# Hybrid decoder trunk step: queries in residue, block and run order, K of the dense head group stored by blocks

## The chip, the cores and the metric

The kernel runs on the 8 NeuronCores of one Trainium2 chip. Every core works on two of the sixteen prompt sequences and on four of the thirty-two one-token samples, with no exchange between cores. The metric is the device time of the slowest core, in microseconds (us). A core has a matrix engine (TensorE: PE in the rows, PEld for its weight loads), VectorE (DVE), ScalarE (ACT), GpSimd (POOL) and SyncE (SP, which here only starts DMA transfers).

## The reference, cut to what matters

One layer: half a SwiGLU step, a mixing step, half a SwiGLU step, a final norm. The mixing step projects h = RMSNorm(x) once to a pooling input, to queries, keys and values of three head groups (four heads of 64 each) and to two gates.

```python
ATTN_GROUPS = ((128, 1), (512, 4), (2048, 16))  # (window, dilation)
q = apply_rope(qkv[:, :, g, 0], pos); k = apply_rope(qkv[:, :, g, 1], pos); v = qkv[:, :, g, 2]
o, lse = dilated_band_attention(q, k, v, window, dil)   # query t reads t - j*dil, j = 0..window//dil
wts = softmax(lses, axis=0); attn = einsum('gnlh,gnlhd->nlhd', wts, outs)
merged = sigmoid(gate_pool) * (pool @ w_pool_br) + sigmoid(gate_attn) * (attn @ w_attn_br)
x = x + merged @ w_o
```

The three groups of a head slot are merged by their softmax denominators. In the kernel the unnormalised products exp(score) times V of all three groups, and the sums of exp(score), are added up in one numerator and one denominator, and one division ends it.

## The kernel before, in words

**Tiles.** A sequence of 2048 tokens is four tiles of 512 tokens. Two tiles, A and B, make a pair, and the kernel runs four pairs one after the other: first feed-forward step for both, projections (`proj`), attention (`attn`), gates and `w_o`, second feed-forward step for both. Activations lie transposed: channels on the 128 partitions, the 512 tokens of the tile along the free dimension.

**Token order.** The 512 columns do not hold the tokens in their natural order. Column 32r + c holds a token of residue class r (of 16, modulo 16), and within a class the 32 tokens stand as c = 4 * c8 + u, where u (0 to 3) is the block of 128 tokens and c8 (0 to 7) the place of the token in that block's run. In the kernel's words this is the order "r c u". So the 128 tokens of block u stand at every fourth column: u, u+4, u+8, and so on.

**What each group reads.** Head group 0 (dilation 1, the dense group) needs blocks of 128 neighbouring tokens, group 1 (dilation 4) needs 128 columns of one class modulo 4, which stand side by side, group 2 (dilation 16) needs 32 columns of one class modulo 16, also side by side. `col` in `attn` (line 755) says so: a slice with step 4 for group 0, a contiguous slice of 128 for group 1. Group 2 slices in `unit2` by itself.

**Attention.** `unit01` handles two heads of one group against the current or the previous block of keys. It issues 16 score matmuls (4 blocks, 2 halves of the head, 2 heads; K is the stationary operand, Q the moving one, 32 partitions each), ScalarE takes exp of the two banks into `pbuf`, VectorE multiplies by a mask (line 765), then come 8 matmuls with V that add into the numerator bank, and 2 matmuls with ones that add into the denominator bank. `unit2` does the same for group 2. The units of a tile are a generator, and `merge` interleaves them by a table of costs with other matmul work: the attention of tile A with the projection of tile B, the attention of tile B with the gates and `w_o` of tile A. Each engine works through its own queue in program order.

**Rotary step.** `rope_pair` (lines 576 to 585) turns two PSUM banks into two rotated halves on VectorE: four products into `rtmp`, then two sums into `qT`, into `kT0`/`kT1`, or into the float32 buffer `kf` where K is also an output of the kernel (group 2 always, groups 0 and 1 in the last tile of a sequence). From `kf` ScalarE copies into the K buffer (lines 682 and 685) and a DMA stores it. All matmuls are recorded at line 198, whoever issues them, so rows are told apart by tile names: scores read `sb_qT` and `sb_kT`, numerator matmuls `sb_pbuf` and `sb_V`, denominator matmuls `sb_pbuf` and `sb_ones`.

**End of a head pair.** ScalarE takes Ln and Exp of the denominators (lines 857 and 859), VectorE multiplies numerator, 0.5 and reciprocal into `attnT` (line 861). GpSimd computes the pooling branch meanwhile.

Of the kernel before, what the change touches and what calls it, by code (L numbers as in the profile page):

```python
# [215 lines left out]
def build(cfg=CFG):  # L216
# [30 lines left out]
    with K.es:  # L247
# [328 lines left out]
        def rope_pair(bA, bB, seg, outA, outB, t, resA, resB):  # L576
# [64 lines left out]
        def proj(seg, s, t, i, mx, S=None):  # L641
# [25 lines left out]
            def qk(g, isk):  # L667
# [4 lines left out]
                if not isk:  # L672
                    rope_pair(bA, bB, seg, qT[:, 2 * g, :], qT[:, 2 * g + 1, :], rtmp, [qT.r[2 * g]], [qT.r[2 * g + 1]])
                else:
                    kout = (g == 2) or last
                    kres = [kTg[g].r[t if g == 2 else t % 3]]
                    if not kout:
                        rope_pair(bA, bB, seg, kTg[g][:, t % 3, 0, :], kTg[g][:, t % 3, 1, :], rtmp, kres, kres)
                    else:
                        rope_pair(bA, bB, seg, kf[:, 0, :], kf[:, 1, :], rtmp, [kf.r[0]], [kf.r[1]])  # L680
                        if g == 2:
                            act.op(lambda: nc.scalar.copy(out=kT2[:, :, :].rearrange("p a (r t c) -> p a r t c", r=NR, t=NTILE)[:, :, :, t, :],
                                                          in_=kf[:, :, :].rearrange("p a (r c) -> p a r c", c=NI)), reads=kf.r, writes=kres)
                        else:
# [64 lines left out]
        def attn(t, i):  # L749
# [5 lines left out]
            def col(g, u, tt=None):  # L755
                return slice(u, T, 4) if g == 0 else slice(u * 128, (u + 1) * 128)
# [27 lines left out]
            def unit01(g, c, which):  # L784
# [8 lines left out]
                if not units:  # L793
# [6 lines left out]
                scores(bk, [lambda i, b, u=u, tt=tt, ku=ku, ab=ab: (ps[b][:, u * 128:(u + 1) * 128], kb[hr(i), tt % 3, ab, col(g, ku)],  # L800
                                                                   qT[hr(i), 2 * g + ab, col(g, u)], ab == 0, ab == 1)
# [27 lines left out]
            def unit2(c):  # L829
# [15 lines left out]
                for part in range(2):  # L845
# [10 lines left out]
                    if part == 1:  # L856
                        act.op(lambda: nc.scalar.activation(out=rden[c][:, :], in_=ps[denb[c]][:, :], func=AF.Ln), reads=[psr[denb[c]]],
# [404 lines left out]
def _consts():  # L1262
# [4 lines left out]
    for g, o in enumerate(order):  # L1267
        mask01[:, g, 0] = o[:, None] >= o[None, :]
        mask01[:, g, 1] = o[:, None] <= o[None, :]
    mask2 = (_run(np.arange(128) % 32)[:, None] <= _run(np.arange(32))[None, :]).astype(np.float32)  # L1270
# [110 lines left out]
```

How the kernel before makes its waits and increments, by code:

```python
    def wait_tok(self, tok):  # L66
        sem, val = tok
        if sem is self.sem:
            if self.is_pe:
                return
            assert val <= self.cnt, (self.name, val, self.cnt)
        if self.known.get(id(sem), 0) >= val:
            return
        self.eng.wait_ge(sem, val)
        self.known[id(sem)] = val
# [21 lines left out]
    def op(self, fn, reads=(), writes=(), inc=True):  # L97
        self.nops = getattr(self, "nops", 0) + 1
        self.wait_deps(reads, writes)
        ins = fn()
        if inc:
            ins.then_inc(self.sem, 1)
            self.cnt += 1
            tok = (self.sem, self.cnt)
        else:
            tok = (self.sem, self.cnt + 1)
        self.commit(tok, reads, writes)
        return tok
# [1 line left out]
    def dma(self, out, in_, dsem, reads=(), writes=(), **kw):  # L110
        self.wait_deps(reads, writes)
        self.eng.dma_start(out=out, in_=in_, **kw).then_inc(dsem.sem, 16)
        dsem.total += 16
        tok = (dsem.sem, dsem.total)
        self.commit(tok, reads, writes)
        return tok
```

## Time and profile before

| what | us |
|---|---|
| median of 3 runs | 2925.41 (2922.5 to 3424.03) |
| profiled execution, whole | 2923.13 |
| profiled execution, span of the slowest core (core 4) | 2921.9 |
| spans of the eight cores | 2911.1 to 2921.9 |
| TensorE busy on that core | 2815.1 (96%) |
| VectorE busy | 1038.7 (36%) |
| ScalarE busy | 755.7 (26%) |
| GpSimd busy | 331.0 (11%) |

The span is the time from a core's first to its last instruction in one profiled execution, and the whole of that execution is 1.2 us longer. Busy time is summed over a core's instructions. The mean granted TensorE clock of core 4 is 0.987 of full speed. An engine that is busy for a third of the span can still be the one that is waited for in a certain stretch.

### The profile page before, as it was taken

What the parts mean: (1) busy time and instruction counts of PE and PEld (TensorE: products, weight loads), DVE (VectorE), ACT (ScalarE), POOL (GpSimd) and SP (SyncE); (2) the same over time, 40 slices, a digit from 0 to 9 for tenths busy, and PEclk for the clock granted to TensorE, in tenths of its full rate; (3) what the DMA queues carried; (4) which work ended last, traced back from release to release, by engine and by line L of the source; (5) the groups of instructions that cost most, each with busy time, mean ns of one, the idle gap of its engine ahead of it and who ended that gap; (6) DMA issues with size and microseconds to landing.
All of it is one profiled execution on the core that took longest, in us unless ns stands there. A gap on an engine that the chain in (4) does not pass through costs nothing.

```text
span 2921.9 us, 47174 instructions; the slowest of 8 cores (2911.1 to 2921.9 us)
## 1 busy us (share of the span) xinstructions
PE 2815.1 (96%) x16993; PEld 1350.6 (46%) x17306; DVE 1038.7 (36%) x1704; ACT 755.7 (26%) x1340; POOL 331.0 (11%) x448
## 2 busy tenths in 40 slices
PE   7999988999999999999999999999999999999997
PEld 2444544444444455444444445444444445544443
DVE  3212753421241166442142128542124216644112
ACT  2111233312121124421122113432112112442111
POOL 1000620000000044000000007000000004400000
PEclk8999998999999999999999999999999999999999
DMA  9666765765353334343343424344224223433221
GB/s 212 146 150 134 192 150 139 182 171 139 107 173 107 110 125 153 109 146 127 103 152 110 138 80 149 125 131 148 83 75 165 71 89 119 144 118 114 73 75 70
DMA packets 97089, 372.58 MB, mean 128 GB/s; under 512 B 12472, under 2 KB 14168, under 8 KB 93660
## 3 DMA queue, kind: packets, MB, share of 16 engines
q1 hardware_dynamic: 75760, 270.81, 27.7%
q0 software_dynamic: 17648, 86.94, 13.9%
q10 hardware_dynamic: 3456, 11.80, 1.0%
q8 instruction: 145, 2.38, 0.3%
q14 instruction: 80, 0.66, 0.1%
HBM read 342.66 MB, written 99.03 MB: 151 GB/s over the span
## 4 chain that ended last, share of the span: by engine, by line
PE 89%; DVE 4%; issue 3%; DMA 2%; ACT 1%; ACTq 0%; SPq 0%; DVEq 0%; POOL 0%; POOLq 0%
PE ps L198 89%; DMA sb_xT<-x 1%; DVE sb_hT L507 1%; DMA sb_uexs<-spoolT 1%; DVE sb_ystg L507 1%; DMA kp<-sb_kf 1%; DVE sb_rtmp L579 1%; DVE sb_pbuf L765 0%; DVE sb_V L214 0%; DVE sb_kf L579 0%; DVE sb_kf L917 0%; ACT sb_pbuf L761 0%; ACT sb_V L213 0%; DMA sb_kT<-kcs 0%; DVE sb_mergedT L919 0%
## 5 line engine op out<-in xcount | busy, mean ns | idle before, releaser
L198 PE MATMUL ps<-sb_hT,sb_w 128*128 128x512 bf16 x7461 | 1685.2, 381 | 31.6 <-issue 6.3
L198 PEld LDWEIGHTS ps<-sb_hT,sb_w 128*128 128x128 bf16 x7680 | 740.6, 98 | 920.2 <-issue 61.0
L525 ACT ACTIVATE sb_stmp<-ps 128x512 f32<-128x512 f32 x352 | 209.8, 597 | 920.5 <-PE ps L198 871.2
L198 PE MATMUL ps<-sb_actTB,sb_w 128*128 128x512 bf16 x1371 | 316.6, 379 | 1.8
L198 PE MATMUL ps<-sb_actTA,sb_w 128*128 128x512 bf16 x1382 | 316.2, 379 | 1.8 <-DVE sb_actTs L526 0.2
L468 ACT ACTIVATE sb_sq<-sb_xT 128x512 bf16<-128x512 f32 x224 | 139.4, 630 | 666.7 <-DVE sb_xT L570 467.3
L526 DVE TENSOR_TENSOR sb_actTB<-sb_stmp,ps 128x512 bf16<-128x512 f32 x176 | 120.9, 687 | 485.8 <-PE ps L198 472.3
L526 DVE TENSOR_TENSOR sb_actTA<-sb_stmp,ps 128x512 bf16<-128x512 f32 x176 | 119.9, 686 | 421.1 <-PE ps L198 417.1
L570 DVE SCALAR_TENSOR_TENSOR sb_xT<-ps,sb_xT 128x512 f32<-128x512 f32 x128 | 87.8, 690 | 434.3 <-PE ps L198 421.2
L198 PEld LDWEIGHTS ps<-sb_actTA,sb_w 128*128 128x128 bf16 x1408 | 136.9, 98 | 163.7 <-issue 0.2
L198 PEld LDWEIGHTS ps<-sb_actTB,sb_w 128*128 128x128 bf16 x1408 | 136.7, 98 | 163.7
L507 DVE SCALAR_TENSOR_TENSOR sb_hT<-sb_xT,sb_gains,sb_rstd 128x512 bf16<-128x512 f32 x192 | 140.3, 798 | 82.1 <-ACT sb_rstd L499 58.3
L579 DVE TENSOR_TENSOR sb_rtmp<-ps,sb_rope 128x512 f32<-128x512 f32 x192 | 119.6, 678 | 17.6 <-PE ps L198 17.3
L917 DVE SCALAR_TENSOR_TENSOR sb_kf<-sb_kf,ps 128x512 f32<-128x512 f32 x128 | 82.5, 683 | 112.5 <-PE ps L198 104.3
L198 PE MATMUL ps<-sb_mergedT,sb_w 128*128 128x512 bf16 x495 | 118.1, 379 | 4.1 <-issue 1.6
L765 DVE TENSOR_TENSOR sb_pbuf<-sb_pbuf,sb_mask 128x512 bf16<-128x512 bf16 (+2 forms) x152 | 79.3, 538 | 116.1 <-ACT sb_pbuf L761 113.3
L112 POOL DMA_DIRECT2D sb_w<-wch x95 | 50.7, 537 | 577.5 <-PE ps L198 553.1
L112 POOL DMA_DIRECT2D kvs<-c x40 | 19.6, 490 | 828.5 <-PE ps L198 801.9
L198 PE MATMUL ps<-sb_sq,sb_meanm 128*128 128x512 bf16 x252 | 88.6, 385 | 15.9 <-ACT sb_sq L468 10.9
L761 ACT ACTIVATE sb_pbuf<-ps 128x512 bf16<-128x512 f32 (+4 forms) x152 | 81.7, 594 | 57.6 <-PE ps L198 52.6
L198 PE MATMUL ps<-sb_w,sb_hT 128*128 128x256 bf16 x768 | 92.8, 278 | 0.7 <-DVE sb_rtmp L579 0.7
L198 PEld LDWEIGHTS ps<-sb_w,sb_hT 128*128 128x128 bf16 x768 | 77.4, 105 | 14.6 <-issue 4.8
(134 smaller groups left out, 1528.5 us busy)
## 6 DMA issues: line engine op xcount, KB each, us to landing
sb_w<-wscr SPq DMA_DIRECT2D x341, 512.0 KB, 4.0
sb_w<-wch POOLq DMA_DIRECT2D x83, 512.0 KB, 8.3
wscr<-sb_w SPq DMA_DIRECT2D x83, 512.0 KB, 4.5
sb_w<-wscr SPq DMA_DIRECT2D x52, 384.0 KB, 3.5
kvs<-c POOLq DMA_DIRECT2D x32, 511.8 KB, 5.0
y<-sb_ystg POOLq DMA_DIRECT2D x7, 2048.0 KB, 12.1
sb_xT<-x SPq DMA_DIRECT2D x8, 1024.0 KB, 11.9
sb_xT<-x SPq DMA_DIRECT2D x4, 2048.0 KB, 10.8
```

Source lines behind the costliest of these rows:

```text
L112: self.eng.dma_start(out=out, in_=in_, **kw).then_inc(dsem.sem, 16)
L198: self.pe.op(lambda: self.nc.tensor.matmul(out, lhsT, rhs, start=start, stop=stop, **kw), reads=reads, writes=writes, inc=inc)
L468: act.op(lambda: nc.scalar.activation(out=sq[:, 0:n], in_=seg.xT[:, c, 0:n], func=AF.Square), reads=[seg.xT.r[c]], writes=sq.r)
L507: dve.op(lambda c=c: nc.vector.scalar_tensor_tensor(out=dst[:, c, 0:n], in0=seg.xT[:, c, 0:n], scalar=gains[:, gi, c:c + 1], in1=seg.rstd[ ...
L525: act.op(lambda: nc.scalar.activation(out=st[:, 0:n], in_=ps[bg][:, 0:n], func=AF.Silu), reads=[psr[bg]], writes=st.r)
L526: dve.op(lambda: nc.vector.tensor_tensor(out=seg.actT[:, j, 0:n], in0=st[:, 0:n], in1=ps[bu][:, 0:n], op=ALU.mult), reads=st.r + [psr[bu]] ...
L570: dve.op(lambda: nc.vector.scalar_tensor_tensor(out=seg.xT[:, m, 0:n], in0=ps[b][:, 0:n], scalar=0.5, in1=seg.xT[:, m, 0:n], op0=ALU.mult, ...
L579: tt = lambda o, a, b, op, rd, wr: dve.op(lambda: nc.vector.tensor_tensor(out=o, in0=a, in1=b, op=op), reads=rd, writes=wr)
L761: act.op(lambda: nc.scalar.activation(out=pb[0:rows, c0:c1], in_=ps[b][0:rows, c0:c1], func=AF.Exp, scale=0.125), reads=[psr[b]], writes=pb.r)
L765: dve.op(lambda: nc.vector.tensor_tensor(out=pv, in0=pv, in1=mask.unsqueeze(1).broadcast_to(list(pv.shape)), op=ALU.mult), reads=pb.r + mr ...
L917: dve.op(lambda: nc.vector.scalar_tensor_tensor(out=gt[:, k, 0:n], in0=gt[:, k, 0:n], scalar=1.0, in1=ps[bk][:, 0:n], op0=ALU.add, op1=ALU ...
```

## The change

The queries of all three groups are written in the order "r u c" (class, block, place in the run) instead of "r c u". K of group 0 is written in the order "u r c", so each block of 128 tokens is contiguous; K of groups 1 and 2 stay as they were. The numerator and denominator banks therefore have their columns in the order "r u c". The last VectorE operation of a head pair writes `attnT` back in the order "r c u", so that everything behind attention is as before. The factor 0.5 moves into the Ln (scale 2.0). The masks of group 1 and 2 are renumbered on the query side. The number of instructions changes only where K of group 0 goes through `kf` (the last tile of each sequence): one ScalarE copy of 1024 columns becomes two of 512.

```diff
+        nat = lambda ap: ap.rearrange("p (r c u) -> p r c u", c=8, u=4)
+        def rope_pair(bA, bB, seg, outA, outB, t, resA, resB, order=None):
...
+            pi = nat if order else (lambda ap: ap)
+            po = (lambda ap: ap.rearrange("p (%s) -> p r c u" % order, c=8, u=4)) if order else pi
...
-            tt(outA, t[:, 0, 0:n], t[:, 1, 0:n], ALU.subtract, [t.r[0], t.r[1]], resA)
-            tt(outB, t[:, 2, 0:n], t[:, 3, 0:n], ALU.add, [t.r[2], t.r[3]], resB)
+            tt(po(outA), pi(t[:, 0, 0:n]), pi(t[:, 1, 0:n]), ALU.subtract, [t.r[0], t.r[1]], resA)
+            tt(po(outB), pi(t[:, 2, 0:n]), pi(t[:, 3, 0:n]), ALU.add, [t.r[2], t.r[3]], resB)
...
-                    rope_pair(..., qT[:, 2 * g, :], qT[:, 2 * g + 1, :], rtmp, ...)
+                    rope_pair(..., qT[:, 2 * g, :], qT[:, 2 * g + 1, :], rtmp, ..., "r u c")
...
-                        rope_pair(..., kTg[g][:, t % 3, 0, :], kTg[g][:, t % 3, 1, :], rtmp, kres, kres)
+                        rope_pair(..., kTg[g][:, t % 3, 0, :], kTg[g][:, t % 3, 1, :], rtmp, kres, kres, "u r c" if g == 0 else None)
...
+                        elif g == 0:
+                            for ab in range(2):
+                                act.op(lambda: nc.scalar.copy(out=kT0[:, t % 3, ab, :].rearrange("p (u r c) -> p r c u", c=8, u=4), in_=nat(kf[:, ab, :])), ...)
...
-            def col(g, u, tt=None):
-                return slice(u, T, 4) if g == 0 else slice(u * 128, (u + 1) * 128)
+            def col(ap, g, u):
+                return ap.rearrange("p (r u c) -> p u r c" if g == 0 else "p (u r c) -> p u r c", u=4, c=8)[:, u]
...
-                        K.mm(ps[numb[c]][64 * i:64 * i + 64, col(g, u)], vs[k][0][:, h * 64:(h + 1) * 64], pbs[i][:, u * 128:(u + 1) * 128],
+                        K.mm(col(ps[numb[c]][64 * i:64 * i + 64, :], g, u), vs[k][0][:, h * 64:(h + 1) * 64], col(pbs[i][:, :], 1, u),
...
-                    den = den.rearrange("p (i u) -> p u i" if g == 0 else "p (u i) -> p u i", u=4)[:, u0:u1, :]
+                    den = den.rearrange("p (r u c) -> p u r c" if g == 0 else "p (u r c) -> p u r c", u=4, c=8)[:, u0:u1]
...
-                        dve.op(lambda: nc.vector.scalar_tensor_tensor(out=attnT[:, c, :], in0=ps[numb[c]][:, :], scalar=0.5, in1=rden[c][:, :], ...
+                        dve.op(lambda: nc.vector.tensor_tensor(out=attnT[:, c, :].rearrange("p (r c u) -> p r u c", c=8, u=4),
+                                                               in0=tok(ps[numb[c]][:, :]), in1=tok(rden[c][:, :]), op=ALU.mult),
```

In bytes along a partition: the moving Q of a group 0 score was read at a step of 8 bytes, and is now read in runs of 8 columns (16 bytes) every 64 bytes; the stationary K was loaded at a step of 8 bytes, and is now contiguous; the numerator and denominator of group 0 were written in PSUM at a step of 16 bytes (one float32 each), and are now written in runs of 8 float32 (32 bytes) every 128 bytes. On VectorE, consecutive bf16 elements of a query sum now go 16 bytes apart (they were 2 bytes apart), those of a group 0 K sum 256 bytes apart, and those of `attnT` 8 bytes apart.

No instruction changes its place; what changes is the form in which operands are walked. VectorE, the rotary step of tile A of the first pair, in which q0, k0 (`sb_kT_22`), q1, k1 and so on follow each other:

```order
-L579 TENSOR_TENSOR sb_rtmp<-ps,sb_rope 128x512 x4
-L579 TENSOR_TENSOR sb_qT_94<-sb_rtmp 128x512 x2
-L579 TENSOR_TENSOR sb_kT_22<-sb_rtmp 128x512 x2
-L579 TENSOR_TENSOR sb_kT_23<-sb_rtmp 128x512 x2
+L584 TENSOR_TENSOR sb_rtmp<-ps,sb_rope 128x512 x4
+L584 TENSOR_TENSOR sb_qT_94<-sb_rtmp 128x16x8x4 x2
+L584 TENSOR_TENSOR sb_kT_22<-sb_rtmp 128x128x4 x2
+L584 TENSOR_TENSOR sb_kT_23<-sb_rtmp 128x512 x2
```

The two sums of each query, and those of K of group 0, are now walked in rows of 4 elements; the products and K of group 1 are as before. TensorE, the numerator and denominator matmuls of one group 0 unit of the same tile:

```order
-L198 MATMUL ps<-sb_pbuf_97,sb_V_25 64x128
-L198 MATMUL ps<-sb_pbuf_98,sb_V_25 64x128
-L198 MATMUL ps<-sb_pbuf_97,sb_ones 64x4x128
+L198 MATMUL ps<-sb_pbuf_97,sb_V_25 64x16x8
+L198 MATMUL ps<-sb_pbuf_98,sb_V_25 64x16x8
+L198 MATMUL ps<-sb_pbuf_97,sb_ones 64x4x16x8
```

Their outputs go in 16 runs of 8 columns for each block. Matmuls of groups 1 and 2 keep their forms.

## Rows read from the trace of the kernel before

**Rows 1.** The page: span, TensorE's busy time, shares of the chain that ended last.
```profile
span 2921.9 us, 47174 instructions; the slowest of 8 cores (2911.1 to 2921.9 us)
PE 2815.1 (96%) x16993; PEld 1350.6 (46%) x17306; DVE 1038.7 (36%) x1704; ACT 755.7 (26%) x1340; POOL 331.0 (11%) x448
PE 89%; DVE 4%; issue 3%; DMA 2%; ACT 1%; ACTq 0%; SPq 0%; DVEq 0%; POOL 0%; POOLq 0%
```
**Rows 2.** TensorE's timeline: start, us, count; group 0 scores, then group 1 scores.
```profile
1118.18 1.10 PE L198 MATMUL ps<-sb_qT,sb_kT 32*128 32x128 bf16 x16
...
1164.19 0.62 PE L198 MATMUL ps<-sb_qT,sb_kT 32*128 32x128 bf16 x16
```
**Rows 3.** TensorE's timeline: numerator and denominator of group 0, then of group 1.
```profile
1160.07 0.63 PE L198 MATMUL ps<-sb_pbuf,sb_V 128*64 128x128 bf16 x8
1160.49 0.64 PE L198 MATMUL ps<-sb_pbuf,sb_ones 128*64 128x512 bf16 x2
1161.06 1.90 PE L198 MATMUL ps<-sb_hT,sb_w 128*128 128x512 bf16 x8
...
1173.07 0.41 PE L198 MATMUL ps<-sb_pbuf,sb_V 128*64 128x128 bf16 x8
1173.32 0.38 PE L198 MATMUL ps<-sb_pbuf,sb_ones 128*64 128x512 bf16 x2
1173.64 1.90 PE L198 MATMUL ps<-sb_hT,sb_w 128*128 128x512 bf16 x8
```
**Rows 4.** VectorE's groups by form, whole span: count, busy us, mean ns.
```profile
L919 DVE TENSOR_TENSOR sb_mergedT<-sb_kf 128x512 bf16<-128x512 f32 x64 | 44.3, 692 | 8.1 <-DVE sb_kf L917 3.2
L579 DVE TENSOR_TENSOR sb_qT<-sb_rtmp 128x512 bf16<-128x512 f32 x48 | 43.3, 941 | 0.0
L579 DVE TENSOR_TENSOR sb_kT<-sb_rtmp 128x512 bf16<-128x512 f32 x24 | 32.9, 1372 | 1.2
L579 DVE TENSOR_TENSOR sb_kf<-sb_rtmp 128x512 f32<-128x512 f32 x24 | 16.0, 706 | 0.0
L526 DVE TENSOR_TENSOR sb_actTs<-sb_stmps,ps 128x4 bf16<-128x4 f32 x44 | 6.8, 155 | 4.1 <-ACT sb_stmps L525 4.0
```
**Rows 5.** The query sums alone: duration ns min/median/max.
```profile
L579 DVE TENSOR_TENSOR sb_qT<-sb_rtmp x48: 670/708/1797, 301.4 to 2535.6; 128x512 bf16<-128x512 f32 x48
```
**Rows 6.** VectorE's timeline, projection of tile A, second pair; brackets: idle before, releaser.
```profile
1065.05 2.47 DVE L579 TENSOR_TENSOR sb_rtmp<-ps,sb_rope 128x512 f32<-128x512 f32 x4
1067.44 1.41 DVE L579 TENSOR_TENSOR sb_qT<-sb_rtmp 128x512 bf16<-128x512 f32 x2
...
1080.72 3.16 DVE L579 TENSOR_TENSOR sb_kT<-sb_rtmp 128x512 bf16<-128x512 f32 x2
...
1093.72 1.28 DVE L579 TENSOR_TENSOR sb_kf<-sb_rtmp 128x512 f32<-128x512 f32 x2
1097.33 0.92 DVE L765 TENSOR_TENSOR sb_pbuf<-sb_pbuf,sb_mask 128x512 bf16<-128x512 bf16 x2 [2.32 <-ACT sb_pbuf L761]
```
**Rows 7.** GpSimd's timeline beside it.
```profile
1080.81 6.17 POOL L615 TENSOR_TENSOR sb_wtmp<-sb_wtmp 128x896 f32<-128x896 f32 x3
```
**Rows 8.** ScalarE's timeline behind it.
```profile
1095.09 1.05 ACT L682 CAST sb_kT<-sb_kf 128x1024 bf16<-128x1024 f32 x1 [6.82 <-DVE sb_kf L579]
1096.62 1.10 ACT L761 ACTIVATE sb_pbuf<-ps 128x512 bf16<-128x512 f32 x2
```
**Rows 9.** TensorE's timeline behind it: two group 0 scores, then the numerator.
```profile
1091.10 1.10 PE L198 MATMUL ps<-sb_qT,sb_kT 32*128 32x128 bf16 x16
1093.97 1.11 PE L198 MATMUL ps<-sb_qT,sb_kT 32*128 32x128 bf16 x16
1098.49 0.63 PE L198 MATMUL ps<-sb_pbuf,sb_V 128*64 128x128 bf16 x8 [1.58 <-DVE sb_pbuf L765]
```
**Rows 10.** Waits of TensorE for masks: us in total, times, longest us.
```profile
PE ps L198 <- DVE sb_pbuf L765: 18.6, 8, 8.2
```
**Rows 11.** VectorE and TensorE in the projection of tile B: mask, then its numerator.
```profile
1131.40 1.22 DVE L765 TENSOR_TENSOR sb_pbuf<-sb_pbuf,sb_mask 128x512 bf16<-128x512 bf16 x2
...
1134.11 0.63 PE L198 MATMUL ps<-sb_pbuf,sb_V 128*64 128x128 bf16 x8
```

More of the change, by code:

```diff
@@ L672, in qk @@
                 if not isk:
[L673 removed]
+                    rope_pair(bA, bB, seg, qT[:, 2 * g, :], qT[:, 2 * g + 1, :], rtmp, [qT.r[2 * g]], [qT.r[2 * g + 1]], "r u c")
                 else:
@@ L677, in qk @@
                     if not kout:
-                        rope_pair(bA, bB, seg, kTg[g][:, t % 3, 0, :], kTg[g][:, t % 3, 1, :], rtmp, kres, kres)
+                        rope_pair(bA, bB, seg, kTg[g][:, t % 3, 0, :], kTg[g][:, t % 3, 1, :], rtmp, kres, kres, "u r c" if g == 0 else None)
                     else:
@@ L683, in qk @@
                                                           in_=kf[:, :, :].rearrange("p a (r c) -> p a r c", c=NI)), reads=kf.r, writes=kres)
+                        elif g == 0:
+                            for ab in range(2):
+                                act.op(lambda: nc.scalar.copy(out=kT0[:, t % 3, ab, :].rearrange("p (u r c) -> p r c u", c=8, u=4), in_=nat(kf[:, ab, :])),
+                                       reads=kf.r, writes=kres)
                         else:
@@ L799, in unit01 @@
                 cc[0] = c
-                scores(bk, [lambda i, b, u=u, tt=tt, ku=ku, ab=ab: (ps[b][:, u * 128:(u + 1) * 128], kb[hr(i), tt % 3, ab, col(g, ku)],
-                                                                   qT[hr(i), 2 * g + ab, col(g, u)], ab == 0, ab == 1)
+                scores(bk, [lambda i, b, u=u, tt=tt, ku=ku, ab=ab: (col(ps[b][:, :], 1, u), kb[hr(i), tt % 3, ab, ku * 128:(ku + 1) * 128],
+                                                                   col(qT[hr(i), 2 * g + ab, :], g, u), ab == 0, ab == 1)
                             for (u, tt, ku) in units for ab in range(2)], kres + qT.r[2 * g:2 * g + 2])
@@ L856, in unit2 @@
                     if part == 1:
-                        act.op(lambda: nc.scalar.activation(out=rden[c][:, :], in_=ps[denb[c]][:, :], func=AF.Ln), reads=[psr[denb[c]]],
+                        act.op(lambda: nc.scalar.activation(out=rden[c][:, :], in_=ps[denb[c]][:, :], func=AF.Ln, scale=2.0), reads=[psr[denb[c]]],
                                writes=rden[c].r)
@@ L860, in unit2 @@
                                writes=rden[c].r)
-                        dve.op(lambda: nc.vector.scalar_tensor_tensor(out=attnT[:, c, :], in0=ps[numb[c]][:, :], scalar=0.5, in1=rden[c][:, :],
-                                                                      op0=ALU.mult, op1=ALU.mult), reads=[psr[numb[c]], ] + rden[c].r,
-                               writes=[attnT.r[c]])
+                        tok = lambda ap: ap.rearrange("p (r u c) -> p r u c", c=8, u=4)
+                        dve.op(lambda: nc.vector.tensor_tensor(out=attnT[:, c, :].rearrange("p (r c u) -> p r u c", c=8, u=4),
+                                                               in0=tok(ps[numb[c]][:, :]), in1=tok(rden[c][:, :]), op=ALU.mult),
+                               reads=[psr[numb[c]]] + rden[c].r, writes=[attnT.r[c]])
                         K.give(denb[c])
@@ L1266, in _consts @@
     mask01 = np.zeros((128, 2, 2, 128), np.float32)
[L1267 to L1270, printed above, removed]
+    qorder = (order[0], 4 * (pos % 32) + pos // 32)
+    for g, (o, q) in enumerate(zip(order, qorder)):
+        mask01[:, g, 0] = o[:, None] >= q[None, :]
+        mask01[:, g, 1] = o[:, None] <= q[None, :]
+    mask2 = (_run(np.arange(128) % 32)[:, None] <= np.arange(32)[None, :]).astype(np.float32)
     half = 32
```

3 lines of the change are left out of this document (1 added, 2 removed).

## The prediction

> **What bounds the kernel now.** I read the page first. TensorE is busy for 2815.1 of 2921.9 us, and the chain that ended last runs through it for 89% [rows 1]. So time on TensorE counts one for one nearly everywhere, and time on another engine counts only where TensorE is seen to wait for it. Next I read TensorE's timeline in the attention stretches, because the change touches only attention. Two units that do the same arithmetic on the same shapes have different lengths there. Sixteen score matmuls of the dense group take 1.10 us, sixteen of group 1 take 0.62 [rows 2]. Eight numerator and two denominator matmuls take 0.99 us of the engine in the dense group (1160.07 to 1161.06) and 0.57 in group 1 (1173.07 to 1173.64) [rows 3]. The only difference between the two is how operands and outputs are walked. Last I read who keeps TensorE waiting. Masks do so 8 times, for 18.6 us [rows 10], and I followed one of these back through ScalarE to VectorE [rows 6, 8, 9], since VectorE is where the change adds work.
>
> **TensorE's part.** A full dense unit can save 1.10 - 0.62 = 0.48 us in its scores [rows 2] and 0.99 - 0.57 = 0.42 us in numerator and denominator [rows 3], together 0.90. There are 8 tiles, 2 head pairs and 2 kinds of unit (current and previous block), so 32 units. In the first tile of each of the two sequences the previous block is missing for one of four blocks: 4 units are three quarters long. That makes 28 x 0.90 + 4 x 0.75 x 0.90 = 27.9 us at full recovery. Whether recovery is full the trace does not show, since no row has runs of 8. The lower bound is nothing: runs with gaps could be as slow as single columns with gaps. The upper bound is group 1's price, as the arithmetic is the same and group 1's operands have no gaps. I take the upper bound. K is now exactly as contiguous as in group 1, a run of 8 touches no more memory words than the same 8 columns without gaps do, if words are 16 bytes of Q or 32 bytes of PSUM wide or less, and the matmuls before touched several times as many. The skill speaks partly against it: the Trainium skill, Advanced Engine Details and Errata, section Memory Cachelines, says that any PSUM pattern that is not contiguous slows matmuls much, and a line later that pairs of neighbours are enough. The first of these sentences would leave the 0.42 in place, which is a rival below.
>
> **What of it is not seen in the end.** In each pair two dense score units stand right before the place where TensorE waits for a mask that is late for another reason [rows 9]. Being through 2 x 0.48 = 0.96 us sooner there only lengthens the wait of 1.58. This pattern occurs four times, once a pair, and the longest mask wait, 8.2 us in the first pair [rows 10], also stands behind two dense score units. Five times 0.96 is 4.8 us. What remains is 27.9 - 4.8 = 23.1 us.
>
> **VectorE's part.** The 48 query sums and 12 of the sums into K (group 0, the six tiles that are not last) are written with gaps, and 16 attnT products. In length they stay 512 elements. What a write with gaps costs on VectorE no row shows. A contiguous sum of two float32 operands into bf16 takes 692 to 708 ns [rows 4, 5]; the same with four columns takes 155, so the 512 elements account for about 540. The lower bound of the added cost is 0 (the engine handles one element at a time in float32, whatever the addresses; the same sum with a float32 output, twice the bytes, takes 706, so written bytes are not its limit) [rows 4]. The upper bound by the longest such row is 1797 ns [rows 5], or 1.09 us more. That one waited for something, so I keep it as an end only. I take 0, because the price of these sums has so far followed the element count alone.
>
> Why this matters although VectorE is busy for 36% only: in the projection of tile A it works without a gap from the first product at 1065.05 to the end of the kf sum at 1095.00, 40 instructions; its first idle time is in front of the mask at 1097.33 [rows 6]. Behind the kf sum wait ScalarE's copy of K (6.82 us idle before it) and, in ScalarE's queue behind that copy, the exps of the two dense units [rows 8], behind them the masks, and behind these TensorE [rows 9]. So there every ns added to VectorE reaches TensorE. Eight permuted sums stand in that stretch (six of queries, two of K of group 0), in each of four pairs: 32 sums. In the other stretches there is cover: in the projection of tile B a mask is ready at 1132.62 and used at 1134.11 [rows 11], 1.49 us later, and two sums more expensive by up to 0.7 us each stay within it. In the gates there are no such sums. If the cover of 1.49 were gone, each us would count there too, in 6 to 8 sums a pair.
>
> **The rest.** attnT: same count, contiguous reads, one instruction per head pair, 8 bytes step; the scalar 0.5 moves into an activation that is there anyway: 0. Two ScalarE copies of 512 instead of one of 1024, twice in the kernel: one fixed cost each, below 0.2 us, in a queue that idles. Masks and DMAs are the same in number and size. SP's and POOL's queues are passed by nothing. A slower VectorE sum holds up GpSimd and the reverse: the K sums into bf16 average 1372 ns against 692, and the one at 1080.72 (3.16 us for two) ran beside GpSimd's additions [rows 4, 6, 7]. That is there before, and it only grows if the sums do.
>
> **Sum.** 2923.1 (the profiled execution) - 23.1 = 2900.0. The median of the runs is 2.3 us above that execution, so the forecast for the median is **2902 us**.
>
> **The rivals.**
> *Half rate on VectorE.* Writes of single bf16 elements 16 bytes apart run at half rate: 0.54 us more each. For it: TensorE shows in the same memory that gaps nearly double a pass (1.10 against 0.62). Against it: TensorE handles a column in far less time than VectorE an element, so memory may keep up with VectorE. In the 32 sums without cover that is 32 x 0.54 = 17.3 us, so 2902 + 17 = 2919. The Trainium skill, Advanced Engine Details and Errata, section Memory Cachelines, speaks for this: it wants two hits in every 16 byte line of SBUF, and a query sum now has one. No run here shows it yet. By the same sentence Q read at 8 bytes had its two hits and should have been fast; the dense scores cost 1.10, so either K's load was slow or the rule is too kind.
> *Runs in PSUM stay slow.* Only the scores recover: 30 or so units x 0.48 = 14.9, less 4.8: 10.1 us, so 2915; if the scores stay slow as well, 2925.
> *Slower than before.* VectorE becomes the bound of the tile A projection: each sum takes two more passes of 0.54, so 1.08 more. The 32 sums cost 34.6 us; in tile B's projection 2.16 per query exceeds the cover of 1.49 by 0.67, some 12 times, 8 us; the sum is 2902 + 43 = 2945. The point from which this side decides is 23.1 / 32 = 0.72 us more per sum. For it: the stretch has no slack at all, and longer sums also hold up GpSimd. Against it: nothing in the trace is three times as slow for its addresses alone.
>
> **Chances and range.** Forecast (VectorE within 0.15 us of its old price, full recovery) 46%, 2897 to 2907. Half rate 28%, 2914 to 2924. Runs in PSUM stay slow, wholly or in part, 14%, 2909 to 2925. Slower than before 10%. Something else 2%. A range of 2896 to 2926 leaves out the slower case and a little at both ends. The lower end is full recovery with a little less lost in waits. A measurement of this kernel can tell about 2% (58 us) from no change. The whole dense excess is 27.9 us, so faster by over 2% needs something not seen here: 1%. Slower by over 2% needs more than 2.5 us per uncovered sum: 2%. Within 2%: 97%.
>
> **What would show it.** In the trace of the changed kernel, dense scores should take 0.62 for sixteen, and numerator plus denominator 0.57; 0.99 there means runs in PSUM stay slow. The query sums should have a median near 708 ns and the tile A projection of the second pair should reach its kf sum 30 us after the first product; near 1250 ns, and 34 us, it is the half rate. The mask wait behind it should be about 2.5 us instead of 1.58 if VectorE is unchanged. I am wrong if query sums exceed 1.4 us, or if TensorE's waits for masks grow beyond some 45 us in all.

## The result: 2.7% slower, and the profile after

The changed kernel takes 1.0268 times as long as before (95% interval 1.0245 to 1.0292): about 3002 us against a median of 2924.7, so some 78 us more where I forecast 23 less. Two of its four executions (3240.9 and 3419.0 us) had one die at a clock of 0.82 to 0.89, which happens to the kernel before too (3424.0); the ratio leaves such executions out.

The page of the changed kernel, to be held against [rows 1]:
```profile
span 3001.5 us, 47178 instructions; the slowest of 8 cores (2993.2 to 3001.5 us)
PE 2815.0 (94%) x16993; PEld 1343.8 (45%) x17306; DVE 1146.2 (38%) x1704; ACT 761.0 (25%) x1342; POOL 380.7 (13%) x448
PE 84%; DVE 7%; issue 5%; ACT 2%; DMA 2%; SPq 0%; DVEq 0%; ACTq 0%; POOL 0%; POOLq 0%
```
TensorE is as busy as before (2815.0 against 2815.1), so all of the 79.6 us show as idle time of TensorE: 106.8 before (2921.9 - 2815.1), 186.5 now. (Why its busy time did not fall is a question of its own, answered below.) VectorE is busy for 107.5 us more.

Did TensorE's walks get faster? Its timeline in two stretches at full clock: sixteen scores of group 0, then numerator and denominator of group 0 and the projection behind them, to be held against the group 0 rows of [rows 2, 3]:
```profile
1145.64 0.62 PE L198 MATMUL ps<-sb_qT,sb_kT 32*128 32x128 bf16 x16
...
1170.81 0.41 PE L198 MATMUL ps<-sb_pbuf,sb_V 128*64 128x128 bf16 x8
1171.06 0.38 PE L198 MATMUL ps<-sb_pbuf,sb_ones 128*64 128x512 bf16 x2
1171.38 1.90 PE L198 MATMUL ps<-sb_hT,sb_w 128*128 128x512 bf16 x8
```
Yes, as forecast: scores 0.62 for 1.10, numerator and denominator 0.57 (1170.81 to 1171.38) for 0.99. By form the three groups fell from 52.7, 32.1 and 31.3 us to 41.5, 26.2 and 24.7: 23.7 us in all.

VectorE, grouped by form, and the query sums alone (ns min/median/max), against [rows 4, 5]:
```profile
L584 DVE TENSOR_TENSOR sb_qT<-sb_rtmp 128x512 bf16<-128x512 f32 x48 | 124.0, 2776 | 0.0
L584 DVE TENSOR_TENSOR sb_kT<-sb_rtmp 128x512 bf16<-128x512 f32 x24 | 53.8, 2242 | 1.2
L872 DVE TENSOR_TENSOR sb_attnT<-ps,sb_rden 128x512 bf16<-128x512 f32 x16 | 21.2, 1326 | 30.8 <-ACT sb_rden L869 30.7
```
```profile
L584 DVE TENSOR_TENSOR sb_qT<-sb_rtmp x48: 2387/2627/4072, 302.0 to 2618.9; 128x512 bf16<-128x512 f32 x48
```
The shortest query sum takes 2387 ns, above every one of before (670 to 1797). These three groups carry 80.7 + 20.9 + 10.2 us more (attnT, the last VectorE operation of a head pair, was 11.0 us, 689 ns each).

Who keeps TensorE waiting (us in total, times, longest), against [rows 10]:
```profile
PE ps L198 <- DVE sb_rtmp L584: 50.9, 17, 9.1
PE ps L198 <- DVE sb_pbuf L775: 23.0, 9, 9.0
PE ps L198 <- DVE sb_attnT L872: 14.9, 10, 4.3
...
PE ps L198 <- ACT sb_pbuf L771: 7.8, 3, 3.9
PE ps L198 <- ACT sb_kf L913: 7.1, 5, 4.4
```
In the kernel before these were 3.6, 18.6, none, 0.2 and 5.0, so they grew by 47.3, 4.4, 14.9, 7.6 and 2.1: 76.3 of the 79.7 us by which TensorE's idle time grew. The first is not the wait that I had followed. sb_rtmp is the output of the rope products, and they are what reads the projection out of its PSUM bank. Behind a long sum the products come late, the banks stay taken, and TensorE has nowhere to write.

The same place as in [rows 6, 9], the tile A projection of the second pair. VectorE:
```profile
1078.80 2.47 DVE L584 TENSOR_TENSOR sb_rtmp<-ps,sb_rope 128x512 f32<-128x512 f32 x4
1081.20 4.76 DVE L584 TENSOR_TENSOR sb_qT<-sb_rtmp 128x512 bf16<-128x512 f32 x2
...
1088.17 5.93 DVE L584 TENSOR_TENSOR sb_kT<-sb_rtmp 128x512 bf16<-128x512 f32 x2
...
1103.24 4.49 DVE L584 TENSOR_TENSOR sb_kT<-sb_rtmp 128x512 bf16<-128x512 f32 x2
1107.66 2.47 DVE L584 TENSOR_TENSOR sb_rtmp<-ps,sb_rope 128x512 f32<-128x512 f32 x4
...
1119.85 1.28 DVE L584 TENSOR_TENSOR sb_kf<-sb_rtmp 128x512 f32<-128x512 f32 x2
```
TensorE beside it:
```profile
1110.27 1.01 PE L198 MATMUL ps<-sb_qT,sb_kT 32*128 32x128 bf16 x15 [4.72 <-DVE sb_rtmp L584]
1111.21 3.59 PE L198 MATMUL ps<-sb_hT,sb_w 128*128 128x512 bf16 x8
1114.74 1.03 PE L198 MATMUL ps<-sb_qT,sb_kT 32*128 32x128 bf16 x16
1120.46 3.19 PE L198 MATMUL ps<-sb_hT,sb_w 128*128 128x512 bf16 x7 [4.69 <-DVE sb_rtmp L584]
1124.63 0.64 PE L198 MATMUL ps<-sb_pbuf,sb_V 128*64 128x128 bf16 x8 [0.97 <-DVE sb_pbuf L775]
```
From the first product to the end of the kf sum VectorE needs 42.3 us without a gap, 30.0 before: 12.4 more. From each start to the next, 11.3 of them stand in the eight permuted sums, and 1.3 in the two sums of K of group 1, whose form did not change (4.49 at 1103.24, 3.16 before [rows 6]). GpSimd, which works beside them, is busy for 380.7 us in the whole kernel instead of 331.0: that longer sums would hold GpSimd up as well was in the prediction. TensorE stops twice, until a product frees a bank (the first time at 1107.66 + 2.47 = 1110.13, and it goes on at 1110.27). The mask at the end, which I had expected to carry the cost, is waited for by 0.97 us only: the time has been lost ahead of it. The second effect stands between the stops: eight 512-column matmuls take 3.59 us, where eight of the same shape take 1.90 in [rows 3]. The windows of that stretch (us, PE, PEld, DVE, ACT, POOL busy, TensorE clock, DMA share, GB/s) show why, first two of after, then one of before around the same place (it begins further ahead of the first product):
```profile
1076.00:1126.00 50.00, 39.16 (x235) 21.83 (x237) 46.70 (x46) 10.66 (x20) 34.83 (x29) 0.86 0.38 126
1110.27:1114.74 4.47, 4.47 (x24) 1.78 (x25) 4.47 (x2) 0.00 (x0) 0.84 (x1) 0.50 0.00 0
```
```profile
1057.00:1100.00 43.00, 41.05 (x262) 24.13 (x266) 39.69 (x52) 11.58 (x22) 32.12 (x34) 1.00 0.49 164
```
After the 4.72 us stop the granted clock is 0.50, the lower of the two levels (1.2 GHz). Behind the stop of 1.58 us in the kernel before [rows 9] it stayed at 1.00. Over the whole kernel the mean clock of a core was 0.987 at least, and is now 0.975 at most. So 22.0 of the 23.7 us that TensorE saved were spent again as slower matmuls (the hT,w group 1685.2 → 1702.6 us, w,hT 92.8 → 97.4), which is why its busy time did not move.

### The profile page after: what moved, and what is told of

The parts are those of the page before. It is cut to its first block, busy times and chain, and to the rows that moved or that the text cites. A ratio compares the mean times of both kernels' runs of the same rounds, so it can differ in the third digit from the quotient of the medians.

```text
span 3001.5 us, 47178 instructions; the slowest of 8 cores (2993.2 to 3001.5 us)
## 1 busy us (share of the span) xinstructions
PE 2815.0 (94%) x16993; PEld 1343.8 (45%) x17306; DVE 1146.2 (38%) x1704; ACT 761.0 (25%) x1342; POOL 380.7 (13%) x448
## 4 chain that ended last, share of the span: by engine, by line
PE 84%; DVE 7%; issue 5%; ACT 2%; DMA 2%; SPq 0%; DVEq 0%; ACTq 0%; POOL 0%; POOLq 0%
PE ps L198 84%; DVE sb_rtmp L584 1%; DVE sb_hT L507 1%; DVE sb_qT L584 1%; DVE sb_pbuf L775 1%; DMA sb_uexs<-spoolT 1%; DVE sb_ystg L507 1%; DVE sb_kT L584 1%; DMA kp<-sb_kf 0%; DMA sb_xT<-x 0%; DVE sb_V L214 0%; DVE sb_attnT L872 0%; ACT sb_pbuf L771 0%; DVE sb_kf L928 0%; DVE sb_kf L584 0%
## 5 line engine op out<-in xcount | busy, mean ns | idle before, releaser
L198 PE MATMUL ps<-sb_hT,sb_w 128*128 128x512 bf16 x7461 | 1702.6, 384 | 52.4 <-DVE sb_rtmp L584 19.5
L584 DVE TENSOR_TENSOR sb_qT<-sb_rtmp 128x512 bf16<-128x512 f32 x48 | 124.0, 2776 | 0.0
L198 PE MATMUL ps<-sb_qT,sb_kT 32*128 32x128 bf16 (+4 forms) x1968 | 62.9, 202 | 41.9 <-DVE sb_rtmp L584 25.0
L198 PE MATMUL ps<-sb_w,sb_hT 128*128 128x256 bf16 x768 | 97.4, 286 | 2.5 <-DVE sb_rtmp L584 2.5
```

The costliest lines, as they stand in the source:

```text
L198: self.pe.op(lambda: self.nc.tensor.matmul(out, lhsT, rhs, start=start, stop=stop, **kw), reads=reads, writes=writes, inc=inc)
```

## The experiments

My theory after the result: a bf16 write on VectorE whose neighbours in time lie 16 bytes apart costs 1.7 us more per 512 elements, and the sums alone make the loss. Rivals: the many short rows of the access pattern cost it (each row now has 4 elements); or something else in the change (K's copies, attnT, the new matmul walks) does.

**e1_forms: each form by itself.** The kernel before, with 17 forms in a row behind its end, four times:
```diff
+        for _ in range(4):
+            dve.op(... tensor_tensor(out=oo, in0=tA_, in1=tB_, op=ALU.add))                  # contiguous
+            dve.op(... out=P(oo, "c r u", "r c u"), in0=P(tA_, "r c u", "r c u"), ...)       # rows of 4, neighbours
+            dve.op(... out=P(oo, "r u c", "r c u"), in0=P(tA_, "r c u", "r c u"), ...)       # rows of 4, 16-byte step
+            ...
```


> The kernel before, with a list of VectorE and ScalarE instructions of 512 elements in different walks put behind its end, four times over, when no other engine works (its total time is not of interest; what it adds after the end belongs to no output). Two theories of why a query sum went from 0.70 to 2.4 us at least. Step theory: a bf16 element that is written alone, 16 bytes or more from the last, costs some 3.4 ns more; the length of a row does not matter. Then rows of 64 elements with a 16 byte step take 2.4 us as well, rows of 128 with an 8 byte step about 1.3, and rows of 4 whose elements are neighbours stay at 0.69. Row theory: every innermost row costs some 13 ns to set up, whatever its steps. Then rows of 4 neighbours take 2.4 us, rows of 8 neighbours 1.5, and long rows with any step stay at 0.69. Permuted reads with contiguous writes: the step theory leaves open what reads cost, the row theory says 1.5 us in rows of 8.


Measured (ns min/median/max; in order: contiguous; rows of 4 neighbours; the query form; 8-byte step; 4-byte step; inputs read at a 16-byte step; float32 written at a 32-byte step):
```profile
L1247 DVE TENSOR_TENSOR sb_kT<-sb_rtmp x4: 693/694/694, 2913.0 to 2986.2; 128x512 bf16<-128x512 f32 x4
L1248 DVE TENSOR_TENSOR sb_kT<-sb_rtmp x4: 692/692/693, 2913.8 to 2987.0; 128x512 bf16<-128x512 f32 x4
L1250 DVE TENSOR_TENSOR sb_kT<-sb_rtmp x4: 2385/2385/2387, 2915.3 to 2988.6; 128x512 bf16<-128x512 f32 x4
L1252 DVE TENSOR_TENSOR sb_kT<-sb_rtmp x4: 1296/1296/1300, 2920.4 to 2993.6; 128x512 bf16<-128x512 f32 x4
L1253 DVE TENSOR_TENSOR sb_kT<-sb_rtmp x4: 727/727/729, 2921.8 to 2995.0; 128x512 bf16<-128x512 f32 x4
L1255 DVE TENSOR_TENSOR sb_kT<-sb_rtmp x4: 1062/1062/1062, 2925.1 to 2998.3; 128x512 bf16<-128x512 f32 x4
L1258 DVE TENSOR_TENSOR sb_kf<-sb_rtmp x4: 1065/1065/1067, 2928.8 to 3002.0; 128x512 f32<-128x512 f32 x4
```
Short rows cost nothing (692), so that rival is dead. The 16-byte step costs 1.69 us, as the step theory had it, and a larger step no more: two further forms, rows of 64 at 16 bytes and rows of 4 at 256 bytes, took 2.42 and 2.43. It is the same on ScalarE (16-byte step, then contiguous):
```profile
L1261 ACT CAST sb_kT<-sb_rtmp x4: 2416/2416/2416, 2931.6 to 3004.8; 128x512 bf16<-128x512 f32 x4
L1262 ACT CAST sb_kT<-sb_rtmp x4: 617/617/617, 2934.1 to 3007.3; 128x512 bf16<-128x512 f32 x4
```

**e2_plain_writes and e3_only_query_writes: the two halves of the change.** e2 keeps every new matmul walk and writes contiguously (K's copy and attnT too); e3 is the kernel before, with the new rope writes only.
```diff
 # e2, against the changed kernel
-            pi = nat if order else (lambda ap: ap)
-            po = (lambda ap: ap.rearrange("p (%s) -> p r c u" % order, c=8, u=4)) if order else pi
+            pi = lambda ap: ap
+            po = pi
 # e3, against the kernel before
-            tt(outA, t[:, 0, 0:n], t[:, 1, 0:n], ALU.subtract, ...)
+            tt(po(outA), pi(t[:, 0, 0:n]), pi(t[:, 1, 0:n]), ALU.subtract, ...)
```


> The changed kernel, with all permuted writes of VectorE and ScalarE (query sums, K sums and copies of group 0, attnT) made contiguous again; TensorE's operand walks stay those of the change. It leaves out the reordering, so columns are mixed up among tokens. My theory (the whole loss comes from the permuted VectorE writes, TensorE's gain is real): about 2900 us, the 23.1 us of the prediction below before. Rival (the changed TensorE walks cost something by themselves, in waits or in the granted clock): 2920 us or above.

> The kernel before, with only the permuted VectorE sums of the change (48 of queries, 12 of K of group 0), TensorE's walks as before. It leaves the attention blocks mixed up among tokens. My theory: the two parts add up, so about 2925 + 78 + 23 - 5 = some 3015 to 3025 us (attnT's permuted write, 16 times 0.64 us, is not in it). Rival (the loss needs the faster TensorE, whose gain turns into waits): below 3005 us.


e2: 0.9952 (0.9935 to 0.9970), 14 us faster. e3: 1.0293 (1.0268 to 1.0318), some 85 us slower. Both lie between what I had expected (2900 and 3015 to 3025) and the rival's limit (2920 and 3005). 85 - 14 = 71 of the 78. The other 7 were not taken apart: attnT (16 x 0.64 = 10 us of VectorE) and the ScalarE copies of K, which neither run has, are what is left of the change. So the writes alone are the loss, and the matmul walks alone a gain, of half the size that I had summed. e2's busy times and waits show where the other half went:
```profile
PE 2788.0 (96%) x16993; PEld 1333.8 (46%) x17306; DVE 1040.8 (36%) x1704; ACT 753.6 (26%) x1342; POOL 331.3 (11%) x448
...
PE ps L198 <- DVE sb_pbuf L775: 21.1, 10, 8.3
...
PE ps L198 <- DVE sb_rtmp L584: 9.8, 8, 1.8
...
PE ps L198 <- ACT sb_kf L913: 7.2, 6, 2.7
```
TensorE is busy for 27.1 us less than before, close to the 27.9 of full recovery. The change has the same matmuls in the same forms and is busy for 2815.0, so 27.0 us of its time are lower clock. The three waits are 2.5, 6.2 and 2.2 us above before, 10.9 in all, where I had put 4.8, and only in front of masks. A TensorE that is through sooner also finds PSUM banks still taken. In front of the mask of the second pair it waits for 2.58 us, where I had forecast 2.5, and what follows is slower than in [rows 9]:
```profile
1089.11 3.11 PE L198 MATMUL ps<-sb_hT,sb_w 128*128 128x512 bf16 x8
```
There the granted clock is 0.58 (1088.12 to 1092.15), where it was 1.00 before.

**e4_read_side: the gap moved from the write to the read.** The sum reads its float32 products at a 16-byte step and writes without gaps. attnT is reordered on its read side too; the ScalarE copies of K stay as in the change.
```diff
-            pi = nat if order else (lambda ap: ap)
+            pi = (lambda ap: ap.rearrange("p (r c u) -> p r u c", c=8, u=4)) if order else (lambda ap: ap)
```


> The changed kernel, with the reordering moved from the write side to the read side on VectorE: sums and attnT are written contiguously in the new order, and their float32 inputs are read in rows of 8 with a 16 byte step (K of group 0 and queries), attnT in rows of 4 with a 32 byte step; ScalarE's two copies of K as in the change. Step theory, if only writes suffer: 2900 us. Row theory: query sums in rows of 8 cost 64 rows x 13 ns = 0.85 us more instead of 1.72, so about half of the loss: near 2945 us. If reads suffer like writes: 3000 us.


1.0039 (1.0025 to 1.0053), 11 us slower than before, 25 slower than e2. A query sum is 1052 ns at best and 1103 in the median, so +0.37 (e1) instead of +1.69, and 67 of the 78 us are back. None of the three times that I had written down (2900, 2945, 3000) came true: a read with gaps costs something, but a fifth of what the write costs. TensorE's wait for rtmp is 19.1 us.

**e6_tile_a_only and e7_tile_b_only: where the sums count.** e2, with permuted sums in one tile's projection only.
```diff
-                    rope_pair(..., [qT.r[2 * g]], [qT.r[2 * g + 1]], "r u c")
+                    rope_pair(..., [qT.r[2 * g]], [qT.r[2 * g + 1]], "r u c" if i == 0 else None)   # e7: i == 1
```


> The changed kernel, with permuted VectorE writes only in the projection of tile A (32 sums), all others plain; it leaves part of the reordering out, so columns are mixed up. My theory (in this stretch VectorE has no slack, every us of a sum reaches TensorE): 2909 us of the plain kernel + 32 x 1.75 = 56, and some more for TensorE's clock after the longer waits: 2965 to 2980 us. Rival (cover exists here too, for instance because TensorE works ahead by several banks): 2940 us or less.

> The changed kernel, with permuted VectorE writes only in the projection of tile B, all others plain; it leaves part of the reordering out. My theory: two sums are 3.5 us more expensive, the cover is about 1.5, so 2 us for each of three or four pairs of sums in four stretches, 24 to 32 us: 2933 to 2941 us. Rival (no cover at all): 2909 + 28 x 1.75 = 2958 us.


e6: 1.0108 (1.0088 to 1.0128), 2955.7, so 46 above e2, less than the 56 and more that I expected: 32 sums x 1.69 = 54 with 8 covered. The wait for rtmp is 49.8 us, so it is tile A's sums that make the 50.9 of the change. e7: 1.0068 (1.0049 to 1.0088), 2943.5, 34 above e2 and 2.5 above the range that I gave: 28 sums x 1.69 = 47 with 13 covered. 2909 + 46 + 34 = 2989; the 13 up to 3002 are attnT, the copies and what the parts do to each other. Tile A was the larger part, as I had argued, but tile B's projection, to which I gave a cover of 1.49 us [rows 11], is no refuge: one mask's slack is not the slack of the stretch. In e7 it is attnT (9.3 us), rtmp (11.2) and ScalarE's pbuf (7.8 in one wait) that TensorE waits for.

**e12_half_dose: the price against the dose.** The same number of sums, written at an 8-byte step (1.30 us each).
```diff
-            po = (lambda ap: ap.rearrange("p (%s) -> p r c u" % order, c=8, u=4)) if order else pi
+            po = (lambda ap: ap.rearrange("p (a b) -> p b a", b=4)) if order else pi
```


> The kernel with plain writes, but query sums and K sums of group 0 written at a step of 8 bytes in rows of 128, which costs 1.30 us per sum alone instead of 0.69 (the change's form costs 2.39). It leaves the reordering out. If the loss is the price of these sums and nothing else, it follows the dose: tile A alone lost 46 us and tile B alone 34 us for 1.70 us per sum, so 0.61 us per sum lose 0.61/1.70 x 80 = 29 us where no cover is used up, and less by what tile B's cover of 1.49 takes: 2925 to 2938 us. Rival (what hurts is the permuted pattern itself, or TensorE's clock falls only beyond long waits): 2920 us or less.


1.0039 (1.0027 to 1.0051), 2935.9, within the expected 2925 to 2938: by the ratios 25 above e2 for +0.61 a sum (60 x 0.61 = 37), against the 46 + 34 = 80 of e6 and e7 for +1.69 (60 x 1.69 = 101). So 0.7 and 0.8 of what is added arrives: between these doses the cost is nearly proportional, and even the small one is not hidden.

**e5_pe_forms and e9_pe_forms_warm: which gap slowed TensorE.** e5 put matmul and VectorE forms behind the end of the kernel before. e9 repeats the matmul part, with eight full matmuls ahead of each form.
```diff
+            for _ in range(8): pe.op(... matmul(ps[bb_[2]][:, :], ones[:], mvv))              # e9 only
+            for u, ab, i in L16: M(... matmul(o_(i, u), kk(i)[:, u:T:4], qq(i)[:, u:T:4]))    # K and Q with gaps; then each alone
+            ...
```


> The kernel before, with a list of matmuls behind its end that isolate the operand walks (16 scores of 32x128 for each of: K and Q at step 4, Q alone at step 4, K alone at step 4, Q in runs of 8, nothing with gaps; 16 denominator matmuls of 512 columns for each of: no gaps, PSUM at step 4, at step 2, in runs of 8), and of VectorE and ScalarE instructions that read PSUM or SBUF in gaps and write without (its total time is not of interest; what it adds belongs to no output). What is open is which operand made the dense scores slow. Line theory (memory is reached in lines of 16 bytes, and the cost is lines touched): Q at step 4 touches 64 lines per matmul, in runs of 8 it touches 16 like without gaps, so Q alone at step 4 takes the whole 0.48 us more and K alone at step 4 nothing much, or the reverse if loads are what counts; Q in runs of 8 costs nothing. In PSUM: step 4 about 1.8 times as long as no gaps, step 2 between, runs of 8 like no gaps. On VectorE, a read at a step of 16 bytes should cost what the sums read in permuted order cost, 1.06 us, from SBUF; from PSUM it may be free (0.68) or not.

> The kernel before, with the list of matmul walks once more behind its end, without waits between them, each group of 16 behind eight plain matmuls, so that TensorE stays at its higher clock (its total time is not of interest). Line theory for the dense scores: Q at step 4 alone 1.04 us for sixteen, K at step 4 alone 0.55, Q in runs of 8 0.55, nothing with gaps 0.55. Rival: K at step 4 alone carries the 0.48, Q alone 0.55. Denominators, sixteen of 512 columns in pairs: no gaps some 1.8 us, PSUM at step 4 3.4 or more, at step 2 the same as no gaps if lines of 8 bytes with two hits are enough, runs of 8 as no gaps.


In e5, where TensorE stood for 0.48 us between the forms, the granted clock was neither level throughout (0.82 from 2920 to 3003): 16 scores without any gap took 1.03 us, those with gaps in Q 1.08 to 1.11, so its TensorE part is inconclusive. Its VectorE part is clear: a product that reads PSUM in the new order costs what a plain one does.
```profile
L1291 DVE TENSOR_TENSOR sb_rtmp<-ps,sb_rtmp x4: 691/692/692, 3003.3 to 3035.3; 128x512 f32<-128x512 f32 x4
L1292 DVE TENSOR_TENSOR sb_rtmp<-ps,sb_rtmp x4: 691/692/692, 3004.1 to 3036.1; 128x512 f32<-128x512 f32 x4
```
e9, in order: scores with gaps in K and Q, in Q alone, in K alone, with Q in runs of 8, with no gaps; then denominators into PSUM with no gaps, at step 4, at step 2, in runs of 8:
```profile
2914.75 1.10 PE L1254 MATMUL ps<-sb_kT,sb_kT 32*128 32x128 bf16 x16
2917.62 1.08 PE L1257 MATMUL ps<-sb_kT,sb_kT 32*128 32x128 bf16 x16
...
2920.47 0.64 PE L1260 MATMUL ps<-sb_kT,sb_kT 32*128 32x128 bf16 x16
2922.87 0.62 PE L1263 MATMUL ps<-sb_kT,sb_kT 32*128 32x128 bf16 x16
...
2925.25 0.62 PE L1266 MATMUL ps<-sb_kT,sb_kT 32*128 32x128 bf16 x16
2927.63 1.92 PE L1269 MATMUL ps<-sb_kT,sb_ones 128*64 128x512 bf16 x16
...
2931.31 3.62 PE L1272 MATMUL ps<-sb_kT,sb_ones 128*64 128x512 bf16 x16
2936.70 3.62 PE L1275 MATMUL ps<-sb_kT,sb_ones 128*64 128x512 bf16 x16
...
2942.09 1.92 PE L1278 MATMUL ps<-sb_kT,sb_ones 128*64 128x512 bf16 x16
```
The scores' excess came from Q's step alone. K by blocks gained 0.02 us a unit at most, and its permuted sums and copies were paid for nothing. Runs of 8 are as fast as no gaps, in SBUF and in PSUM.

**e8_psum_read, e10_queries_from_psum, e11_tables_by_sync: a version that gains.** If the order is made where it is free (the products read PSUM in the new order and write without gaps), the sums stay plain. The tables must then be in the new order too. e8 does this for queries and K, with a permuted table in the place of two of the four product buffers:
```diff
+            tt(vo(t0), A_, cos, ALU.mult, ...)
+            tt(vo(t1), B_, sin, ALU.mult, ...)
+            tt(outA, t0, t1, ALU.subtract, ...)
+            tt(vo(t0), A_, sin, ALU.mult, ...)
```


> The changed kernel, with the reordering moved to where VectorE and ScalarE read PSUM: the four rotary products read their bank in the new order (runs of 8 at a 16 byte step) against a second table of cosines and sines that is stored in that order, so products, sums and K of group 0 are written contiguously; the Ln of the denominators and the last product of a head pair read PSUM in the old order and write contiguously. The second table takes the room of two of four product buffers, and costs one 512 KB transfer per tile. It computes everything. My theory (VectorE pays for gaps in SBUF, 1.06 us read and 2.4 us written, and nothing for gaps in PSUM, 0.69): the time of the kernel with plain writes, 2909 us, give or take 3. Rival (gaps in PSUM or the closer order of products cost something in company of the other engines): 2925 us or more.


1.0103 (1.0088 to 1.0118), 2956.4: a miss. The products took their 0.69 us, but with two buffers each sum follows its own products directly, and VectorE idles for 0.10 to 0.17 us in front of it:
```profile
1088.49 1.80 DVE L587 TENSOR_TENSOR sb_kT<-sb_rtmp 128x512 bf16<-128x512 f32 x1 [0.17 <-DVE sb_rtmp L587]
```
From the first product to the end of the kf sum VectorE needed 33.7 us (30.0 before). The wait for rtmp was 41.9 us, 32.1 above e2. 10.2 of them are one stop in the first pair, where the first product waited for the table to land; the other 13 waits have the larger part. No run has one of the two without the other.
e10 keeps four buffers, permutes queries only (K stays as before, by e9) and puts the tables into two idle buffers:
```diff
+            pin = (lambda ap: ap.rearrange("p (r c u) -> p r u c", c=8, u=4)) if new else (lambda ap: ap)
+            tt(pv(t[:, 0, 0:n]), pin(ps[bA][:, 0:n]), cos, ALU.mult, ...)
+                act.dma(rstd[k][:, :], ropeq_d[t, k], ds_rq[k], writes=rstd[k].r)
```


> A version built from the findings: only the queries change order, and they do so where the four rotary products read PSUM (four product buffers as before; the cosines and sines in the new order lie in the two buffers of the norm's reciprocal roots, which are idle then, loaded from ScalarE's queue; tile B's norm uses a pooling buffer instead). K of all groups stays as before the change, read at step 4 by the weight loads, since K's step cost TensorE nothing. The last product and the Ln read PSUM in the old order and write contiguously. It computes everything. My theory: TensorE's part of the change at no cost on VectorE, as the kernel with plain writes, so a ratio of about 0.995 to the kernel before, 2908 to 2912 us. Rival (the table's transfers or the closer buffers bring a wait of their own, as in the version before this one): 2920 us or more.


1.0011 (1.0001 to 1.0021), median 2925.7 against 2923.1: a miss again, nothing gained. ScalarE, in front of the exp that the mask and TensorE wait for:
```profile
1092.09 2.78 ACTq L112 DMA_DIRECT2D sb_rstd<-ropeq  x2
1095.08 0.59 ACT L665 COPY sb_uext<-ps 128x512 f32<-128x512 f32 x1 [2.88 <-issue]
...
1097.43 0.64 PE L198 MATMUL ps<-sb_pbuf,sb_V 128*64 128x128 bf16 x8 [5.54 <-DVE sb_pbuf L779]
```
Two DMA issues, right behind the two that store K and V, held ScalarE's queue for 2.8 us (2.4, 2.8, 2.3 and 1.4 in the four pairs), where TensorE waits behind it. The two for tile A of the same pair, which stand elsewhere, took 0.83 (1046.54). e11 moves those of tile B to SyncE:
```diff
-            load_ropeq(tB)
+            load_ropeq(tB, sp)
```


> The version before this one (queries reordered where PSUM is read, K as before), with the two table transfers of tile B issued from SyncE's queue instead of ScalarE's. In its trace these two issues held ScalarE up for 2.8 us right ahead of the exps that TensorE waits for, once a pair. My theory: 4 x 2.8 = 11 us come back, so 2911 to 2916 us. Rival (the issues were not what was waited for): 2925 us again.


0.9976 (0.9966 to 0.9987), median 2915.7 against 2924.1: 8 us faster than before (7 by the ratio), 86 faster than the change, and inside the expected 2911 to 2916. TensorE's wait for masks fell from 29.9 to 21.3 us. It beats both kernels.

## Why the prediction was wrong

- **TensorE's part: right.** 0.62 and 0.57 at full clock, as forecast, e2 saves 27.1 of the 27.9 us of busy time, and e9 shows why: runs of 8 cost what no gaps do. The rival that runs in PSUM stay slow is dead. The sentence of the Trainium skill that spoke for it (Advanced Engine Details and Errata, Memory Cachelines: any PSUM pattern that is not contiguous slows matmuls much) does not hold for runs of 8 (1.92 against 1.92), and the one behind it, that pairs of neighbours are enough, is not contradicted by step 2, which has no pairs (3.62).
- **What of it is not seen: too small.** 4.8 us were taken off the 27.9. With cheap writes 14 us remain, so 14 went. In e2 TensorE's idle time grew by 12.1 us (from 106.8 to 118.9), 10.9 of it in the three waits.
- **VectorE's part: this is the step that failed.** "I take 0, because the price of these sums has so far followed the element count alone." The measured price is 1.69 us alone and 2.63 against 0.71 in the median in place. The bounds failed as well: I drew the upper end (1.09) from the longest contiguous sum, which had waited for something, a row that holds no write with gaps at all. Elements had always been contiguous in those rows, so the count explained them all; that is no evidence on addresses. My lower bound (one element at a time, "whatever the addresses") says only that a gap cannot make the sum faster. The trace did hold one instruction class with and without gaps, TensorE's, nearly doubled by them, and I used it for the half rate only. The Trainium skill, Advanced Engine Details and Errata, Memory Cachelines, warned in kind: a line of 16 bytes wants two hits, a query sum has one. e1 agrees and goes further: at an 8-byte step, with two elements in each line, a sum still costs 1.30. So of my two readings of the dense scores (K's load was slow, or the rule is too kind) e9 leaves the second: Q at the same step costs 1.08 for 0.62.
- **Why it matters: the place was right, the route partly wrong.** The uncovered stretch is the tile A projection, and it grew by 12.4 us in the second pair. But the cost reached TensorE through PSUM banks that the products free late (+47.3 us), not through K's copy, exp and mask (+4.4).
- **Cover in tile B: wrong.** 34 us arrived there (e7), where the slower rival had 8.
- **The rest, priced at 0: wrong, smaller.** attnT costs 0.64 more each, and a ScalarE copy at a 16-byte step 2.42 instead of 0.62 (e1). Together with what the parts do to each other they make about 13 us (3002 - 2989).
- **The rival "slower than before"** had the right mechanism and threshold form (0.72 a sum), but 1.08 for the price and 2945 for the time. With 1.69 in it, its own sum gives 2902 + 54 = 2956 from tile A, and a cover of 1.49 against 3.4 per query pair, 12 times, 23 more: 2979. The 23 us up to 3002 are, by the runs, 7 of matmul gain that did not come (2909 for 2902), 11 in tile B (34 for 23) and 13 of the rest, less 8 in tile A (46 for 54). My falsifier on the query sums (over 1.4 us) came true, the one on mask waits (45 us) did not (23.0).

## What to carry to other kernels

A rearrangement that lets TensorE read in runs must be paid by somebody: price the scattered write before anything else, since on VectorE and ScalarE it can cost more than three times the plain one, and look for a stage at which the order is free (here a read of PSUM). Durations of contiguous rows bound nothing about rows with gaps. Where an engine is 36% busy but works without a break in one stretch, two thirds to five sixths of what is added to it there came out at the end (25 of 37, 34 of 47 and 46 of 54 us), and a long stop of TensorE also costs clock afterwards: behind 4.72 and 2.58 us the granted clock was 0.50 and 0.58, behind 1.58 it was 1.00.

## What the runs showed of the hardware that I had not expected

- A bf16 write of 512 elements costs as if by the 16-byte lines that it enters in turn: contiguous 0.69 us, 4-byte step 0.73, 8-byte 1.30, 16-byte 2.39, 256-byte 2.43. Less the 0.155 us that a sum of 4 columns takes [rows 4], the three in the middle are 4.5, 4.5 and 4.4 ns for each of 128, 256 and 512 lines; contiguous, the 512 elements set the time.
- float32 does not follow this price: written 32 bytes apart, which also enters 512 lines, a sum takes 1.07, and with both inputs read at a 16-byte step 1.06. A read of PSUM by VectorE at a 16-byte step costs nothing (0.692 against 0.692).
- On TensorE a step of 8 bytes in the moving operand costs 16 score matmuls 1.08 instead of 0.62, in the stationary operand next to nothing (0.64). In PSUM, writes at 8 and at 16 bytes are equally slow (3.62 for 1.92).
- Two DMA issues in ScalarE's queue took 2.78 us where they stood right behind two others, and 0.83 elsewhere.
